# Two streaming-encoder layers: both SwiGLU FFNs as two half-width passes with one level of Strassen, partial sums seeded in PSUM

## The reference, cut to what matters

```python
def swiglu(h, w_gate_up, w_down):              # h (T, 1024)
    g, up = jnp.split(h @ w_gate_up, 2, -1)    # w_gate_up (1024, 2*2816)
    return (silu(g) * up) @ w_down             # w_down (2816, 1024)

for layer in (0, 1):
    x = x + mixer[layer](rmsnorm(x))
    x = x + swiglu(rmsnorm(x), w_gate_up[layer], w_down[layer])
```

## Time and profile before

| what | value |
|---|---|
| runs shown | 3059.77, 3185.33, 3537.17 us (median 3185.33) |
| profiled execution, slowest core | span 3053.4 us (cores 3034.2 to 3053.4) |
| lowest run less that span | 6.4 us of start and end |
| granted TensorE clock | 0.982 to 0.986 on the 8 cores |
| PE / DVE / ACT / POOL busy | 96% / 40% / 27% / 15% |

### The profile page before, as it was taken

The page is one execution under the profiler, slowest core; times in us unless marked ns, Lnnn a source line. Parts: engine busy times, 40 slices in busy tenths (PEclk is TensorE's granted clock), DMA queues, the critical chain, the costliest instruction groups (busy, mean ns, idle before and its releaser), DMA issues.

```text
span 3053.4 us, 38614 instructions; the slowest of 8 cores (3034.2 to 3053.4 us)
## 1 busy us (share of the span) xinstructions
PE 2923.1 (96%) x15852; PEld 1424.3 (47%) x15852; DVE 1213.0 (40%) x2065; ACT 821.6 (27%) x1582; POOL 450.8 (15%) x912
## 2 busy tenths in 40 slices
PE   6789999799999999999999999997999999999999
PEld 3445555344444444444445555543444444444444
DVE  7668777313212212212366777763221211111111
ACT  2222222112111111111256666766210100100100
POOL 3111112121101100002222333442200000000000
PEclk9889999899999999999999999998999999999999
DMA  9656577995413411305623222374611021021010
GB/s 182 163 134 163 145 179 156 147 139 125 92 33 97 96 29 69 90 15 115 142 46 88 87 90 90 97 162 111 200 65 43 28 68 49 25 66 54 22 57 28
DMA packets 234116, 289.17 MB, mean 95 GB/s; under 512 B 151058, under 2 KB 151586, under 8 KB 233812
## 3 DMA queue, kind: packets, MB, share of 16 engines
q1 hardware_dynamic: 196692, 224.27, 27.6%
q0 software_dynamic: 37248, 62.44, 13.3%
HBM read 202.07 MB, written 114.39 MB: 104 GB/s over the span
## 4 chain that ended last, share of the span: by engine, by line
PE 87%; DMA 4%; DVE 3%; ACT 2%; SPq 1%; issue 1%; POOL 1%; DVEq 0%; POOLq 0%; ACTq 0%
PE ps L636 84%; PE ps L919 2%; DMA WG<-wgu 1%; SPq L666 1%; DMA xr<-xp 1%; DVE Xph L891 1%; DMA hT<-h 1%; ACT tr L591 1%; DMA WiA<-wie 1%; DVE hr L606 0%; ACT ex L1257 0%; DVE xn L615 0%; PE ps L646 0%; ACT L591 0%; ACT hr L591 0%
## 5 line engine op out<-in xcount | busy, mean ns | idle before, releaser
L636 PE MATMUL ps<-hT,WG 128*128 128x512 bf16 x5632 | 1227.4, 380 | 32.6 <-DMA hT<-h 26.9
L636 PEld LDWEIGHTS ps<-hT,WG 128*128 128x128 bf16 x5632 | 551.3, 98 | 701.2 <-issue 22.1
L591 ACT ACTIVATE st<-ps 128x512 f32<-128x512 f32 (+1 forms) x422 | 250.6, 594 | 1456.2 <-PE ps L636 1403.6
L602 DVE TENSOR_TENSOR xr<-ps,xr 128x512 f32<-128x512 f32 (+1 forms) x268 | 173.8, 684 | 582.5 <-PE ps L636 575.6
L602 DVE TENSOR_TENSOR hidD<-ps,st 128x512 bf16<-128x512 f32 x176 | 121.7, 691 | 490.7 <-PE ps L636 483.5
L602 DVE TENSOR_TENSOR hid<-ps,st 128x512 bf16<-128x512 f32 x176 | 121.6, 691 | 460.9 <-PE ps L636 460.9
L636 PE MATMUL ps<-hT,WiA 128*128 128x512 bf16 x1280 | 285.8, 381 | 6.4 <-DVE zb L602 5.1
L636 PE MATMUL ps<-WDc,hidD 128*128 128x512 bf16 x1216 | 267.7, 379 | 0.0
L591 ACT ACTIVATE hr<-xr 128x1024 bf16<-128x1024 f32 x132 | 139.0, 1053 | 445.5 <-DVE xr L602 404.4
L636 PE MATMUL ps<-WDa,hid 128*128 128x512 bf16 x1152 | 253.9, 379 | 0.0
L615 POOL TENSOR_SCALAR msr<-ssr 128x1 f32<-128x1 f32 x132 | 40.2, 305 | 1088.7 <-ACT hr L591 1086.0
(11 more groups left out here) (179 smaller groups left out, 2306.9 us busy)
## 6 DMA issues: line engine op xcount, KB each, us to landing
x<-xr SPq DMA_DIRECT2D x96, 512.0 KB, 3.3
xr<-x SPq DMA_DIRECT2D x96, 512.0 KB, 5.1
xr<-xp SPq DMA_DIRECT2D x64, 512.0 KB, 6.0
h<-hr SPq DMA_DIRECT2D x124, 256.0 KB, 3.3
WG<-wgu POOLq DMA_DIRECT2D x64, 256.0 KB, 12.7
yp<-xr SPq DMA_DIRECT2D x32, 512.0 KB, 2.8
wgb<-wgu POOLq DMA_DIRECT2D x24, 256.0 KB, 8.8
WG<-wgb POOLq DMA_DIRECT2D x12, 512.0 KB, 10.7
```

The source lines that it names most:

```text
L591: return tag(e.activation(out=R(out), in_=R(in_), func=func, **kw))
L602: return P.add(eng, lambda e, tag: tag(e.tensor_tensor(out=R(out), in0=R(a), in1=R(b), op=op)), [a, b], [out], c)
L636: ins = e.matmul(R(out), l, r, start=st, stop=sp_, skip_group_check=True)
```

## The change

Each FFN runs as two passes over all 8 tiles: pass 0 with hidden groups 0 to 5, pass 1 with groups 6 to 10. Pass 0 stores x plus its half into a new HBM buffer (`X[4]`, `X[5]`), pass 1 loads that, adds its half, stores and norms as before. Every product is one level of Strassen in Winograd's form: 7 half-size products in place of 8. For gate/up the halves are taken over the k-chunks and over the tile's columns, and gate and up are the two output halves; for down over the two 128-row chunks of each group, over the tile's rows and over the 512-column output halves.

The sums that the products need are made by DVE in SBUF, all in bf16: of h once per tile and pass (`hsums`, 4 operations of [128, 4, 256]), of `hid` for each one or two groups (`dsums`, 4 operations), of each weight group after its load (`tsums`, 4 for WG and 4 for WD). A running chain `ch` accumulates in one bank; at three points ACT copies it into another bank (`seed`), where a further product adds onto the copy. For that the bank must have been written in full by a matmul before: `schedule` tracks it (`bank_full`) and can insert a dummy matmul (`prime`). A gate/up group is 7 products of 8 matmuls of 256 columns; a down half `u` is 7 products of 6 or 5 matmuls of 512 columns.

Weights of each pass are loaded as its SBUF places come free; all but 3 WG groups come from bf16 copies in HBM, which POOL's DMA casts fill in earlier stages (`cast_some`: during A tiles 2 to 6, both passes of FFN 0, and C). The last attention tile has one gate/up group woven in, where it had 9 to 12 half-group steps.

```diff
-            for part in (range(20), range(20, 22)): ... hid[:, k, c0:c0+128] x wdn(layer, k)
+        def hsums(layer, p):
+            a11, a12, a21, a22 = hT0[:, 0:4, 0:256], hT0[:, 4:8, 0:256], hT0[:, 0:4, 256:512], hT0[:, 4:8, 256:512]
+            tt("dve", s1, a21, a22, ALU.add, fast=True)
+            tt("dve", s2, s1, a11, ALU.subtract, fast=True)
+            tt("dve", a21, a11, a21, ALU.subtract, fast=True)
+            tt("dve", s4, a12, s2, ALU.subtract, fast=True)
+        def gu_unit(layer, p, k, ring):
+            def seed(src):
+                pt = PT(); pt.seed = pt.full = True
+                cpp(pt.v(0, 512), src.v(0, 512))     # ACT copy, PSUM to PSUM
+                return pt
+            ch, e = PT(), PT()
+            prod(ch, 0, a11, True)
+            prod(e, 1, s1, True)
+            b11 = seed(ch)
+            es = ring.next(); cpp(es[:, :], e.v(0, 512))
+            prod(ch, 5, s2, False)
+            prod(b11, 2, a12, False)
+            b12 = seed(ch)
+            prod(ch, 4, s3, False)
+            prod(b12, 3, s4, False)
+            b21 = seed(ch)
+            tt("dve", u2[:, :], ch.v(0, 512), es[:, :], ALU.add)
+            prod(b21, 6, a22, False)
+            act(tm1[:, :], b11.v(0, 512), AF.Silu)
+            tt("dve", es[:, :], b12.v(0, 512), es[:, :], ALU.add)
+            tt("dve", hid[:, 2 * k:2 * k + 2, 0:256], es, tm1, ALU.mult)
+            act(tm2[:, :], b21.v(0, 512), AF.Silu)
+            tt("dve", hid[:, 2 * k:2 * k + 2, 256:512], u2, tm2, ALU.mult)
+        def down(layer, p, t, ring, order):
+            early, late = order[:nk - 2 + nk % 2], order[nk - 2 + nk % 2:]
+            for u in range(2):                       # early groups of both halves
+                prod(ch, u, 0, (0, 0), early, True); prod(e, u, 1, 0, early, True)
+            for u in range(2):
+                x1, x2 = xload(kin, t, u, ring=XF), xload(kin, t, 2 + u, ring=XF)
...
+                # late groups, then seeds and products as in gu_unit; 6 DVE adds into x1, x2
+                for blk, xb in ((u, x1), (2 + u, x2)):
+                    xstore(kout, t, blk, xb)         # or yp in the last pass
+                    if p == 1: norm(kout, t, blk, xb, G[0])
-                fills = fill[:5] + fills + fill[5:9]
+                fills = [lambda: None] + fills + fill[:1]
```

More of the change, by code:

```diff
@@ L27, in __init__ @@
         self.ops = []
+        self.full = False
+        self.seed = False
     def v(self, c0, c1, p0=0, p1=128, bf=False, rr=None, **kw):
@@ L293, in schedule @@
             if best is None:
+                c = [b for b in range(8) if not bank_busy[b] and not bank_full[b]]
+                if c:
+                    op = self.prime(c[0])
+                    for d in bank_last[c[0]]:
+                        op.deps[d] = False
+                    op.start = max(free["pe"], bank_free[c[0]])
+                    op.end = free["pe"] = op.start + op.cost
+                    bank_free[c[0]], bank_last[c[0]], bank_full[c[0]] = op.end + LAT, [op], True
+                    order["pe"].append(op)
+                    commit.append(op)
+                    continue
                 raise RuntimeError("stuck at op %d of %d, free banks %d" % (low, len(ops), nfree))
@@ L629, in mmg @@
             for m in mms:
+                a = m[0]
+                if isinstance(a, PA) and not a.bf and a.c1 - a.c0 == 512 and a.p1 - a.p0 == 128:
+                    a.pt.full = True
                 n = nel(m[0])
@@ L974, in out_proj @@
                 out_tail(kx, t, blk, pts, gain, inter, last)
[L976 to L987, removed]
-                    hooks[n]()
[L990 to L1006, removed]
+        def tsums(w):
+            n = int(np.prod(w.shape[2:]))
+            def f(k):
+                a = w[:, k]
+                return a.rearrange("p a b -> p (a b)") if len(w.shape) == 4 else a
+            for d, a, b in ((4, 3, 1), (1, 1, 0), (5, 3, 1), (6, 2, 5)):
+                tt("dve", f(d), f(a), f(b), ALU.subtract, fast=True)
@@ new lines, in ffn_units, with gu @@
+        def ffn_units(layer, p, t, ring, order, hooks={}):
+            nk = len(order)
+            def gu(n):
+                gu_unit(layer, p, order[n], ring)
+                if n % 2 == 1 or n == nk - 1:
+                    ks = sorted(order[n - n % 2:n + 1])
+                    if ks[-1] - ks[0] == len(ks) - 1:
+                        dsums(layer, p, ks[0], ks[-1] + 1)
+                    else:
+                        for k in ks:
+                            dsums(layer, p, k, k + 1)
+                if n in hooks:
+                    hooks[n]()
+            return [lambda n=n: gu(n) for n in range(nk)] + [lambda: down(layer, p, t, ring, order)]
```

363 lines of the change are left out of this document (276 added, 87 removed).

## The result

The changed kernel takes 2946.34 us (median of four runs, 2944.43 to 2949.80); the kernel before, beside it, 3122.55 (3056.82 to 3537.17). The ratio is 0.9634, 95% interval [0.9615, 0.9653]: 3.7% faster. The forecast was 2885, range 2835 to 3045. Direction and range held, the size did not: from lowest run to lowest run 112.4 us went, where 174.8 were forecast. Some executions are lengthened by a lower clock on one half of the chip; ratios leave them out, and an experiment without a ratio is told by its profiled span.

A forecast was written before the change was run, and what follows sets the result against it. The prediction took PE's matmul columns to bound the FFNs. Product gains of 141.6 and 76.0 us and 20 at FFN 1's entry, less smaller losses, summed to -175.6 from the lowest run, 3059.8: 2885 us, range 2835 to 3045.

The forecast's parts named there:

- tile starts, +30: At 30 FFN tile starts inside stages, transposes and sums mostly covered by down; 1 us each, 30 us lost.
- rival 2: Tile starts uncovered: transposes slow under the casts' traffic, 189 us lost in place of 30, 3044 us; chance 0.13.
- Moved DMA: hidden: Extra store and load of x and second read of h, about 84 MB, hidden at DMA shares of 0.15 to 0.31.
- Products: FFN matmuls on PE: gate/up gains 141.6 us, with 256-column matmuls at 0.109 us; down gains 76.0 us.
- rival 5: Half-width gate/up matmuls cost more than half as weight loads become the bound; break-even 0.123 us, time 3030; chance 0.02.
- Seeds: ACT's copies between PSUM banks in gate/up and down: nearly hidden behind other products, 5 us for both.
- Rival 1: Seeds queue on ACT: 720 seeds each behind one other operation lose 432 us, time 3317; chance 0.12.
- DVE's sums: DVE's added bf16 sums in FFN tiles: 39.8 of 54.8 us in pass 0, 40.7 of 45.6 in pass 1; PE stays the bound.
- Into C: +3: Boundary from FFN 0 into attention stage C: 3 us lost.
- Between the passes, +5 each: Boundary between pass 0 and pass 1, twice, waiting on weights: 5 us lost each.
- the -20 for the entry: Entry into FFN 1 from the last attention tile: overhead falls from 67 to 45 us; 20 us gained, bounds -30 and +10.
- The clock: Rival 4: a tenth of gate/up runs at the lower clock, +107 us, time 2992; chance 0.04.

The follow-up runs named there:

- e11: The kernel before with its FFN 0 weight casts in a DMA stream of their own, two in flight; ratio 1.0070 to the kernel before.
- e3: Changed kernel with weight casts in a DMA stream of their own, two in flight instead of six shared with weight loads; ratio 0.9434, median 2886.55 us.
- e4: Changed kernel with every seed copied twice by ACT; span 2987.5 us.
- e10: e3 with three of the four DVE sums of h and of hid made twice; span 2887.4 us.
- e6: e1 with the load of WoC moved behind the first C tile's input projection; ratio 0.9491 to the kernel before, span 2910.1 us.
- e9: e3 with WoC's load moved behind the first C tile's products and put in the two-deep stream; ratio 0.9406 to the kernel before.
- e1: Changed kernel with each FFN 0 cast tied to the newest DVE operation of its gate/up group; ratio 0.9456 to the kernel before, span 2900.5 us.
- e2: Changed kernel with only the casts of pass 0 tied to DVE operations of their gate/up groups; span 2917.4 us.

## Why the prediction was right and wrong, by its steps

**The step that failed: tile starts, +30.** The sum had 1 us for each of 30 starts, with a bound of 8 "if DMA is loaded"; measured are two starts with waits of 40.23 and 32.99 us, 73.2 together, and little at the others, whose periods are mostly 54.81 and 45.87. What it had wrong is the time of the transposes. It took the 5.83 us of four for all tiles, and put the slow ones, 24.73 for two at FFN 0's start, into rival 2 as something that would hold at fifteen starts of each kind; they took 48.66 and 42.30 us at one start of each pass. Rival 2 had the mechanism, the casts' traffic, but not the places. It should have asked at which starts POOL has DMAs in flight: the second tile of each pass in FFN 0, since the queue runs ahead. The trace of the kernel before held one such group, at the second tile of its FFN 0, where 38 us of down covered it (SP's timeline):

```profile
668.25 21.39 SPq L666 DMA_TRANSPOSE hT<-h  x4
```

A smaller error: the prediction counted all of down as cover, 18.1 and 15.1 us. Cover is only what the planner has put ahead of the waiting instruction. In pass 0 all of it was; but at 1155.99 three down products of five matmuls (3.2 us) still stood behind the product that waited, and in e11 all of a tile's down did. "Moved DMA: hidden" is the same error: a share of 0.15 to 0.31 is a mean, and a burst with a share over 1 says nothing in it. Without the burst the kernel gives what the sum said: e3's span is 174.3 below the kernel before's, 175.6 were forecast, and its median of 2886.55 stands beside 2885. That closeness is in part luck: it holds errors of both signs (table above), and the cores of that execution span 2844.1 to 2879.1.

**Products: right.** -217.6 us forecast; a tile of pass 0 takes 54.81 us by the trace with its sums and seeds, one of pass 1 45.87. So 0.109 us for 256 columns holds, and rival 5 is out. PE's busy time fell by 188.3 only; 7 us of sample products were forecast to come back, and products behind the waits ran at the lower clock, but the difference was not broken down.

**Seeds: small, as forecast, but not for the reason given.** 5 us forecast; 14.6 us of PE waits name ACT's PSUM copies, about 7 of it in the 36 us behind the second big wait, and the groups of the changed kernel show the copy at 583 ns, against 597 taken. But the margin of 0.02 us did not decide: e4 doubles the copy and the period of pass 0 stays. Rival 1 had its chance from that margin and deserved less.

Groups of ACT and DVE in the changed kernel (busy us, mean ns, idle before):

```profile
L639 ACT ACTIVATE ps<-ps 128x512 f32<-128x512 f32 x720 | 419.6, 583 | 458.8 <-PE ps L687 430.2 <-DVE sxA L650 12.0 <-DVE sxC L650 12.0
...
L650 DVE TENSOR_TENSOR hT<-hT 128x1024 bf16<-128x1024 bf16 x32 | 22.1, 690 | 0.0
L650 DVE TENSOR_TENSOR shB<-hidB_ 128x512 bf16<-128x512 bf16 x16 | 6.8, 423 | 0.4
```

**DVE's sums: priced too high.** 1.284 us was taken for 1024 elements and 0.749 for 512; measured are 0.690 and 0.423. DVE has 31.1 us of work in a tile of pass 0 (39.8 forecast) and 32.6 in pass 1 of FFN 0 (40.7 forecast). The Trainium skill ("VectorE: DVE Perf Modes", The perf-mode tier table) gives a bf16 `tensor_tensor` in SBUF two elements a cycle; by that page the prediction had near 34 us for pass 1, and the trace agrees with 32.6. e10 shows that the room was real.

**Boundaries.** Into C: +3, with +6 for casts in A and C together, against +21.3; 10.7 of it is the wait for `svn`, which the POOL queue holds behind WoC's load. e6 and e9 moved that wait without a gain, and e3 has 11.3 there with `svn` at 7.5; what makes up the rest is open. Between the passes, +5 each: in FFN 1 it is 51.13 us from the transposes of pass 1's first tile to those of its second, with 18.1 and 30.5 of products between them, so about 2.5. From C's fourth tile on, 13.9 us more were gained than forecast: the 15 for starts in FFN 1 did not occur, where no casts run and the periods are 54.81 and 45.87. How the rest of that stretch splits, the -20 for the entry among it, was not broken down. ACT's table loads fell from 23 to 5 in the whole kernel, as the step into FFN 1 assumed.

**The clock: right for the changed kernel.** 1.00 in its steady windows, and 0.70 and 0.72 in the two windows of the waits. The Trainium skill ("TensorE: Matmul & The Clock Gate", A second HAM failure mode) tells of a kernel whose clock oscillated as it cycled through PSUM banks; the steady windows of the changed kernel, which cycles them too, do not show that. On the core shown for e3 the clock was lower in some stretches in which PE was busy throughout, and tiles of pass 1 in FFN 0 took 46.7 us there in place of 45.87; no run here shows why. A window of e3, in the columns used above:

```profile
1200.00:1250.00 50.00, 49.97 (x372) 36.75 (x370) 34.36 (x55) 26.92 (x48) 10.87 (x20) 0.95 0.91 201
```

**The base.** The sum was made against the lowest run, 3059.8. The median shown, 3185, is of runs that reach from 3059.77 to 3537.17, so the distance from it to 2885 was never the change's own. Nor did a lifted median of 3010 come: the four runs after lie between 2944.43 and 2949.80.

## What to carry to other kernels

When a change shortens the work that stands ahead of a load, look for what else is in the DMA queues at exactly those moments; a stage's mean share hides a burst. Bound background DMAs by the number in flight, since pacing by program order binds nothing on a queue that has no other work: the two-deep stream makes this kernel 5.7% faster than the one before (0.9434) where the change alone gives 3.7%. And where an order is fixed, read the cover of a late load from the instructions that stand ahead of its first user, not from the work that exists.

## What the runs showed of the hardware that was not expected

Four DMA transposes of a tile's h, 1.05 MB, are issued in 5.2 us at best (e1, e2). Beside cast DMAs from POOL (256 KB written each) the second tiles' took 9 to 11 us with two in flight, 19 to 21 with four and 34 to 49 with six. The Trainium skill ("DMA: Bandwidth & Descriptors", Queues, rings and completion order) says that an engine takes turns between the queues that have work, a packet at a time; by that rule alone one would not expect the time to grow with the number waiting in one queue, and here it grew about fourfold from two to six. What in the queues makes it grow was not tried. During the slow transposes the DMA engines count as fully busy (a share of 1.20) while moving 95 GB/s (640 to 680 us in the changed kernel), less than the 138 that the steady tiles of pass 1 move at a share of 0.46.
